# A bidirectional mLSTM and pooling block on one core: the head of the program rebuilt

## The chip, the cores and the metric

The kernel runs on one core of a Trainium2 chip. The metric is the device time of one execution, in microseconds (us). The engines are TensorE (PE, with PEld for its weight loads), VectorE (DVE), ScalarE (ACT), GpSimd (POOL) and SyncE (SP), which here only issues DMAs.

## The reference, cut to what matters

One layer of a hybrid diffusion backbone is computed in float32 for 128 context tokens and 1024 latent tokens, 1152 in all, of width 1024:

```python
mod = jnp.dot(jax.nn.silu(cond), w_ada) + b_ada
sh1, sc1, gt1, sh2, sc2, gt2 = [m[:, None, :] for m in jnp.split(mod, 6, axis=-1)]
h = _rmsnorm(x, g_pre_mix) * (1 + sc1) + sh1
z = jnp.einsum('bld,de->ble', h, w_in)
q, k, v, o, ig, fg, u, ga, gb = jnp.split(z, IN_SPLIT_POINTS, axis=-1)
log_f = jax.nn.log_sigmoid(fg + b_f)          # and log_i = ig + b_i, per direction and head
...                                            # two mLSTM directions, pooling mixer, merge, w_out
x = x + gt1 * _rmsnorm(y, g_post_mix)
...                                            # ConvFFN with sh2, sc2, gt2
```

`cond` is `c_ctx` for the context tokens and `c` for the latent ones, so `mod` has two columns of 6144 numbers. Nothing of the layer can be multiplied by `w_in` before `sh1` and `sc1` exist, which are the first 2048 numbers of `mod` (16 tiles of 128). The gate rows `ig` and `fg` go through two running scans over all tokens before the mLSTM can start.

## The kernel before, in words

Every large product is made of three matmuls: each float32 operand is split into a high and a low part, and hi·hi, hi·lo and lo·hi are added in PSUM. A **unit** is 128 output columns of a weight: 8 steps over the depth `k`, for 3 blocks of 384 tokens, so 24 steps of three matmuls. ACT makes the high part of a unit's weight (`hi_split`, into `ring_hi`), DVE the low part (`lo_split`, into `ring_lo`), into a ring of 3 slots. The semaphore `lo_ready` counts the low parts, `done0` the blocks that PE has finished, `evac0` the blocks that have been read out of PSUM, and `take0(q)` makes PE wait until the PSUM bank that block `q` writes is free again (`evac0` at least `q - 2`).

The **units in order** are set by the list `mains`: the gates, four of `u` (the pooling mixer's input), two of `v`, then `q` and `k` of head 0; after these nine (`SEG`) the attention of four heads runs between the units that follow. The order within an engine is the order of the code.

The **head** is what runs before unit 0. SP issues all its loads on one queue: the identity, block 0 of x, group 0 of the first modulation columns (`adaw`, 4 groups of 512 columns, 2 MB each, each group as two halves of 4 `k`), 13 small vectors into `vecs` (the last of them `c_ctx` and `c` and the conv weights), groups 1 and 2, blocks 1 and 2 of x, group 3, some constants, then the weights. PE transposes `vecs`, DVE copies the result to `vT`, and ACT takes silu of its last 16 columns as `condT`. PE then holds two columns of `condT` still and streams 512 columns of `adaw` past them (L741, 4 groups of 8), ACT copies each result row to `ada_row`, and 16 narrow transposes (L746) turn the rows into columns of 128 in PSUM bank 7. ACT squares and sums x (`x_stats`, L1098), DVE scales it (`scale_x`, L1451); `first_coef` (L1438, L1440) adds the bias and makes `coefA1`. Only then can ACT read the transposed x out of PSUM with the modulation (L1125, `norm_evac`), and DVE split it into `H_hi` and `H_lo` (L1464, L1401).

Unit 0, the gates, runs block by block while x is transposed for the block after (`first_norm`, L725). ACT then adds the gate bias to its three blocks and takes Abs, Exp and Ln (L1206 to L1212, `log_f_ready`); DVE makes the scans and sums in `gates()` (L1477 to L1511), which ends at `gate_rows_ready`. PE transposes those rows (L871, L873) at the end of unit 2.

The other 32 tiles of the modulation are made later, one to a unit from unit 2 on: DVE multiplies and adds a 128 x 1024 tile of `w_ada` (`ada_products`, L1571 and L1575), and PE sums it over the partitions with two matmuls against `ones` (`ada_sum`, L719) ahead of the unit's own matmuls. The wait of `ada_sum` is

```python
pe.wait_ge(ada_summed, a - ADA0 + 1)
```

and DVE's first such tile is made inside `gates()`, the second after `gates()` has ended.

## Time and profile before

| | us |
|---|---|
| median of 3 runs | 1965.92 (1962.02 to 1967.28) |
| the profiled execution, its span | 1965.6 |
| PE busy in the span | 1897.3 |
| DVE busy | 1026.7 |
| ACT busy | 628.3 |

The execution's own time is its span of 1965.6 us; what lies around it is within 0.4 us of the median. The page of the profile cuts the span into 40 equal slices of 49 us. In the first PE is 6 tenths busy and DVE 1 tenth, in the third PE's granted clock is 9 tenths, and from the fourth to the 39th nearly every slice shows PE at 9 tenths or more. The head and what follows it, up to 117 us, is therefore the part to look at closely.

### The profile page before, as it was taken

The numbers are of one execution on the slowest core, as the hardware profiler recorded it, in microseconds if no ns is written. First come the engines' busy times: TensorE is split into PE (matmuls) and PEld (weight loads), VectorE is DVE, ScalarE is ACT, GpSimd is POOL, SyncE is SP. The second block draws the span as 40 slices with busy tenths as digits, with TensorE's granted clock in tenths as the row PEclk, the third lists the DMA queues.
The fourth block names the chain that finished last, engine by engine and source line by source line (L and its number), as shares of the span: only waits on it lengthen the run. The fifth ranks groups of instructions, "written<-read, shape, count | busy, mean of one in ns | idle before, by whom it ended". The sixth has DMA issues, their size and how long they took to land.

```text
span 1965.6 us, 26936 instructions
## 1 busy us (share of the span) xinstructions
PE 1897.3 (97%) x10465; PEld 1772.4 (90%) x10465; DVE 1026.7 (52%) x2241; ACT 628.3 (32%) x1133; POOL 86.2 (4%) x125
## 2 busy tenths in 40 slices
PE   6999999999999999999999899999999999999995
PEld 1889999999999999999988899989989989989984
DVE  1853555555545333364545555555555555555556
ACT  2723222233234243361334442323223223223222
POOL 1000000000000000010000100000000000000003
PEclk9989999999999999999999899999999999999998
DMA  9133223323333233274222111111111111111104
GB/s 334 33 93 101 71 65 101 98 68 116 100 78 112 87 89 130 87 260 154 93 89 90 61 44 43 44 43 37 48 43 32 51 45 32 43 34 52 43 32 171
DMA packets 165370, 164.41 MB, mean 84 GB/s; under 512 B 5816, under 2 KB 141524, under 8 KB 165284
## 3 DMA queue, kind: packets, MB, share of 16 engines
q1 hardware_dynamic: 150532, 108.36, 18.8%
q0 software_dynamic: 10432, 37.17, 5.4%
q10 hardware_dynamic: 4320, 17.70, 2.2%
q8 instruction: 58, 0.95, 0.2%
q14 instruction: 28, 0.23, 0.0%
HBM read 131.48 MB, written 31.72 MB: 83 GB/s over the span
## 4 chain that ended last, share of the span: by engine, by line
PE 86%; DVE 5%; ACT 3%; issue 3%; DMA 2%; POOL 0%; SPq 0%; DVEq 0%; ACTq 0%; POOLq 0%
PE ps L696 20%; PE ps L698 20%; PE ps L697 20%; PE ps L929 5%; PE ps L1000 3%; PE ps L1002 3%; PE ps L1001 3%; PE ps L809 2%; PE ps L812 2%; PE ps L811 1%; PE ps L741 1%; DMA x1ld<-z_x 1%; PE ps L788 1%; DVE H_lo L1401 1%; ACT Wt L1179 1%
## 5 line engine op out<-in xcount | busy, mean ns | idle before, releaser
L696 PE MATMUL ps<-H_hi,ring_hi 128*128 128x384 f32 x2328 | 798.3, 343 | 5.0 <-DVE H_lo L1401 4.1
L697 PE MATMUL ps<-H_lo,ring_hi 128*128 128x384 f32 x2328 | 781.5, 336 | 0.0
L698 PE MATMUL ps<-H_hi,ring_lo 128*128 128x384 f32 x2328 | 781.4, 336 | 0.0
L696 PEld LDWEIGHTS ps<-H_hi,ring_hi 128*128 128x128 f32 x2328 | 439.7, 189 | 8.3 <-DVE H_lo L1401 4.7
L697 PEld LDWEIGHTS ps<-H_lo,ring_hi 128*128 128x128 f32 x2328 | 439.7, 189 | 1.6
L698 PEld LDWEIGHTS ps<-H_hi,ring_lo 128*128 128x128 f32 x2328 | 439.3, 189 | 0.0
L1771 DVE TENSOR_TENSOR acc<-ps,acc 128x512 f32<-128x512 f32 x198 | 135.0, 689 | 103.1 <-PE ps L1002 103.1
L1401 DVE TENSOR_TENSOR ring_lo<-raw,ring_hi 128x1024 fp32r<-128x1024 f32 (+1 forms) x129 | 152.1, 1188 | 55.4 <-ACT ring_hi L1085 48.1
L1000 PE MATMUL ps<-ring_hi,fT_hi 128*128 128x512 f32 x396 | 157.4, 397 | 12.5 <-DVE acc L1771 10.1
L1001 PE MATMUL ps<-ring_lo,fT_hi 128*128 128x512 f32 x396 | 155.2, 392 | 0.0
L1002 PE MATMUL ps<-ring_hi,fT_lo 128*128 128x512 f32 x396 | 155.1, 392 | 0.0
L1743 DVE SCALAR_TENSOR_TENSOR conv_g<-ps,vT,conv_g 128x378 f32<-128x378 f32 (+2 forms) x176 | 86.1, 510 | 121.9 <-ACT conv_g L1356 117.3
L1545 DVE SCALAR_TENSOR_TENSOR Cst<-Cst,Et,ps 128x257 f32<-128x257 f32 x64 | 30.9, 483 | 222.2 <-PE ps L812 222.2
L1085 ACT ACTIVATE ring_hi<-raw 128x1024 fp32r<-128x1024 f32 x66 | 68.2, 1049 | 214.5 <-PE ps L1002 212.6
L1575 DVE SCALAR_TENSOR_TENSOR ada_part<-raw,condT,ada_part 128x128 f32<-128x128 f32 x448 | 120.3, 344 | 0.0
L1743 DVE SCALAR_TENSOR_TENSOR conv_v<-ps,vT,conv_v 128x378 f32<-128x378 f32 (+2 forms) x176 | 86.1, 510 | 44.9 <-ACT conv_v L1356 40.2
L1000 PEld LDWEIGHTS ps<-ring_hi,fT_hi 128*128 128x128 f32 x396 | 74.7, 189 | 36.5 <-DVE acc L1771 19.0
L456 ACT ACTIVATE stage<-ps 128x384 f32<-128x384 f32 x72 | 35.2, 488 | 211.1 <-PE ps L698 211.1
L1002 PEld LDWEIGHTS ps<-ring_hi,fT_lo 128*128 128x128 f32 x396 | 74.8, 189 | 16.0
L1001 PEld LDWEIGHTS ps<-ring_lo,fT_hi 128*128 128x128 f32 x396 | 74.7, 189 | 14.6
L1057 ACT ACTIVATE ring_hi<-raw 128x1024 fp32r<-128x1024 f32 (+1 forms) x63 | 63.2, 1008 | 75.1 <-PE ps L698 57.3
L1361 ACT ACTIVATE fT_hi<-conv_v 128x384 fp32r<-128x384 f32 x66 | 34.7, 525 | 142.4 <-DVE conv_v L1760 142.4
(232 smaller groups left out, 1951.9 us busy)
## 6 DMA issues: line engine op xcount, KB each, us to landing
raw<-in_w_in_dram SPq DMA_DIRECT2D x44, 512.0 KB, 4.0
raw<-in_w_up_dram SPq DMA_DIRECT2D x44, 512.0 KB, 3.8
raw<-in_w_ada_dram SPq DMA_DIRECT2D x32, 512.0 KB, 5.0
raw<-in_w_down_dram SPq DMA_DIRECT2D x22, 512.0 KB, 3.8
adaw<-in_w_ada_dram SPq DMA_DIRECT2D x8, 1024.0 KB, 13.6
z_o<-stage ACTq DMA_DIRECT2D x8, 576.0 KB, 2.8
z_ga<-stage ACTq DMA_DIRECT2D x8, 576.0 KB, 2.8
z_gb<-stage ACTq DMA_DIRECT2D x8, 576.0 KB, 2.8
```

The lines of the kernel that those rows point to most:

```text
L696: pe.matmul(out, whi, xhi, start=first, stop=False)
L697: pe.matmul(out, whi, xlo, start=False, stop=False)
L698: return pe.matmul(out, wlo, xhi, start=False, stop=last)
L929: mm = pe.matmul(ps[:, bank + hb, :], x[:, k, tok], w[:, hb * 512:(hb + 1) * 512], start=(n == 0 and first), stop=(n == KD - 1 and last))
L1000: pe.matmul(out, fT_hi[:, slot, k, tok], ring_hi[:, r, cols], start=(k == 0), stop=False)
L1001: pe.matmul(out, fT_hi[:, slot, k, tok], ring_lo[:, r, cols], start=False, stop=False)
L1002: mm = pe.matmul(out, fT_lo[:, slot, k, tok], ring_hi[:, r, cols], start=False, stop=(k == 1))
L1085: act.activation(ring_hi[:, r, :], raw[:, n0 % RS, :], ACT.Copy).then_inc(hi_ready, 1)
L1401: return dve.tensor_tensor(out, full, hi.bitcast(F32), ALU.subtract)
L1575: ins = dve.scalar_tensor_tensor(out=part, in0=w, scalar=condT[:, cond, k:k + 1], in1=part, op0=ALU.mult, op1=ALU.add)
L1743: return dve.scalar_tensor_tensor(out=out, in0=src, scalar=vcol(w + NF * half + f, i), in1=out, op0=ALU.mult, op1=ALU.add)
L1771: dve.tensor_tensor(acc[:, t, cols], ps[:, 6 + hb, :], acc[:, t, cols], ALU.add).then_inc(evac2, 1)
```

## The change

The conditioning vectors `c_ctx` and `c` and the identity are loaded first, on ACT's queue, into a tile of their own (`cvec`), and PE transposes these 16 rows alone. SP's loads now go: group 0, x block 0, group 1, eleven vectors, group 2, x block 1, group 3, x block 2.

The groups are divided. **Groups 0 and 2** are multiplied and added by DVE (`ada_group`: 16 operations of 128 x 512 each), and PE sums them over the partitions with 8 matmuls of one column against `ones` (`ada_wide_sums`). **Groups 1 and 3** are made by PE with the 128 x 128 pieces of `adaw` held still and two columns of `condT` streamed (`ada_direct`: 32 matmuls to a group, 16 to a half). The row copies and the narrow transposes are gone.

The first **three units** are now gates, q and k of head 0, in this order (`RU = 3`), and they run block by block: all three for block 0, all three for block 1, all three for block 2. ACT reads them out with `ramp_evac`, and takes Abs, Exp and Ln after block 2 of the gates. The later tiles of the modulation start at unit 3 instead of unit 2, `gates()` takes the first of them, and the gate rows are transposed at the end of unit 4. Both `v` units now stand last before `SEG`, and both of their transposes follow the second (`v_turns`).

```diff
-    mains = [("gates", 0)] + [("u", g) for g in range(4)]
-    mains += [("v", 0), ("v", 1), ("q", 0), ("k", 0)]
+    mains = [("gates", 0), ("q", 0), ("k", 0)] + [("u", g) for g in range(4)]
+    mains += [("v", 0), ("v", 1)]
...
+    RU = 3
-    for s in range(2, NM):
+    for s in range(RU, NM):
...
+    def v_turns(m):
+        before = [mains[m - 1][1]] if m and mains[m - 1][0] == "v" and m != SEG else []
+        return before + ([mains[m][1]] if m == SEG - 1 else [])
...
+    def main_q(m, b):
+        return RU * b + m if m < RU else 3 * use_of[("main", m)] + b
...
+            ada_load(0)
             x_load(0)
-            ada_load(0)
+            ada_load(1)
...
-            for g in range(1, AG):
-                if g == AG - 1:
-                    x_load(1)
-                    x_load(2)
-                ada_load(g)
+            ada_load(2)
+            x_load(1)
+            ada_load(3)
+            x_load(2)
...
             pe.wait_ge(ident_in, 16)
+            pe.wait_ge(cond_in, 32)
+            pe.transpose(ps[:, 2, 0:16], cvec[0:16, :], ident[0:16, 0:16]).then_inc(cond_rows, 1)
...
+            def ada_direct(g, kh):
+                pe.wait_ge(ada_in[2 * g + kh], 16)
+                for a in range(4 * g, 4 * g + 4):
+                    for k in range(kh * KD // 2, (kh + 1) * KD // 2):
+                        mm = pe.matmul(ps[:, 7, 2 * ADA0 * kh + 2 * a:2 * ADA0 * kh + 2 * a + 2],
+                                       adaw[:, g, k, (a % 4) * P:(a % 4 + 1) * P], condT[:, :, k],
+                                       start=(k % (KD // 2) == 0), stop=(k % (KD // 2) == KD // 2 - 1))
+            def ada_wide_sums(g):
+                pe.wait_ge(ada_wide_mac, 2 * KD * (g // 2 + 1))
+                for a in range(4 * g, 4 * g + 4):
+                    for cond in range(2):
+                        mm = pe.matmul(ps[:, 7, 2 * a + cond:2 * a + cond + 1],
+                                       ada_wide[:, g // 2, cond, (a % 4) * P:(a % 4 + 1) * P], ones[:, :], start=True, stop=True)
...
+            for b in range(NB):
+                for m in range(RU):
+                    if b == 0:
+                        pe.wait_ge(lo_ready, m + 1)
+                    take0(main_q(m, b))
+                    for k in range(KD):
+                        if b == 0 and m == 0 and k < KD - 4:
+                            first_norm(0, k + 4)
+                        if b + 1 < NB and m and k % 2 == 0:
+                            if m == 1 and k == 0:
+                                pe.wait_ge(x_scaled, TB * (b + 2))
+                            first_norm(b + 1, (m - 1) * KD // 2 + k // 2)
+                        if m == 0:
+                            pe.wait_ge(h_split_done, b * KD + k + 1)
...
-                if m == 2:
+                if m == RU + 1:
                     pe.wait_ge(gate_rows_ready, 1)
...
             act.wait_ge(coef1, 1)
-            for b in range(NB):
-                norm_evac(lambda w: ps[:, 3 + w % 4, :], lambda w: act.wait_ge(xt_done, w + 1), xt_free, coefA1, 0, 0, tsc, 4, b)
+            first_evac(0)
+            hi_split(1)
+            x_stats(2)
+            hi_split(2)
+            first_evac(1)
+            for m in range(RU):
+                ramp_evac(m, 0)
+            first_evac(2)
+            for m in range(RU):
+                ramp_evac(m, 1)
+            ramp_evac(0, 2)
+            hi_split(3)
...
+            scale_x(0)
+            dve.wait_ge(vec_done, 1)
+            dve.tensor_copy(vT[:, :], ps[:, 1, 0:NV]).then_inc(vec_done, 1)
+            ada_group(2)
+            scale_x(1)
             first_coef()
...
+            norm_split(0, tsc, 4, 0)
+            lo_split(1)
+            scale_x(2)
+            lo_split(2)
+            norm_split(0, tsc, 4, 1)
+            norm_split(0, tsc, 4, 2)
```

**On PE, from the first instruction to the first product of unit 0.** Before (a run of equal rows for `ada_in1` to `ada_in7` stands where the line is left out; `ada_in` counts the halves of the groups):

```order
L711 MATMUL ps<-ident,vecs 128x108 [waits vectors_in,ident_in]
L712 MATMUL ps<-ident,vecs 128x88
L713 MATMUL ps<-ident,vecs 128x88
L741 MATMUL ps<-adaw,condT 2x512 [waits ada_in0,cond_done]
L741 MATMUL ps<-adaw,condT 2x512 x3
...
L746 MATMUL ps<-ident,ada_row 128x2 [waits row_read] x16
L725 MATMUL ps<-ident,X_96 128x128 [waits x_scaled]
```

Now, with L747 `ada_direct`, L757 `ada_wide_sums` and L732 the transposes of x:

```order
L720 MATMUL ps<-ident,cvec 128x16 [waits cond_in,ident_in]
L747 MATMUL ps<-condT,adaw 128x2 [waits ada_in2,cond_done]
...
L765 MATMUL ps<-ident,vecs 128x92 [waits vectors_in]
...
L757 MATMUL ps<-ones,ada_wide 128x1 [waits ada_wide_mac,pool_seq]
...
L732 MATMUL ps<-ident,X_97 128x128 [waits x_scaled]
...
L747 MATMUL ps<-condT,adaw 128x2 [waits ada_in6]
...
L757 MATMUL ps<-ones,ada_wide 128x1 [waits ada_wide_mac]
...
L747 MATMUL ps<-condT,adaw 128x2 [waits ada_in7]
```

The transpose of `vecs` has moved behind all of group 1, and group 3 stands in two halves around the sums of group 2.

**On ACT, from the last reads of the gates to the two functions of their logarithm.** Before:

```order
L1206 ACTIVATE Gt_97<-ps,gbias 36x384 [waits done0]
L1207 ACTIVATE Gt_98<-ps,gbias 36x384
L1210 ACTIVATE Gt_99<-Gt_98 36x1152 [waits evac0]
L1211 ACT_TABLE_LOAD
L1211 ACTIVATE Gt_99<-Gt_99 36x1152 [waits act_seq]
L1212 ACT_TABLE_LOAD
L1212 ACTIVATE Gt_99<-Gt_99 36x1152 [waits act_seq]
L1057 ACTIVATE ring_hi<-raw 128x1024 [waits done0,landed0]
```

Now (the gates' reads are L1170 and L1171, those of q and k L1173 and L1175):

```order
L1173 ACTIVATE qT_66<-ps 128x384 [waits done0]
L1175 ACTIVATE kT_67<-ps 128x384 [waits done0]
L1170 ACTIVATE stage_76<-ps,gbias 36x384 [waits done0]
L1171 ACTIVATE stage_77<-ps,gbias 36x384
L1089 ACTIVATE ring_hi<-raw 128x1024 [waits done0,landed2]
L1192 ACTIVATE Gt_98<-stage_77 36x1152 [waits evac0]
L1193 ACT_TABLE_LOAD
L1193 ACTIVATE Gt_98<-Gt_98 36x1152 [waits act_seq]
L1194 ACT_TABLE_LOAD
L1194 ACTIVATE Gt_98<-Gt_98 36x1152 [waits act_seq]
L1173 ACTIVATE qT_66<-ps 128x384 [waits done0]
```

The logarithm now stands behind the reads of q and k of blocks 0 and 1 and behind one more `hi_split`.

**On DVE, the end of `gates()` and the tile of the modulation that comes after it.** Before:

```order
L1511 CAST YS<-Gt_104 36x1152
L1401 TENSOR_TENSOR GS<-Gt_102,GS 36x1152 [waits dve_seq]
L1401 TENSOR_TENSOR YS<-Gt_104,YS 36x1152
L1571 TENSOR_SCALAR ada_part<-raw,condT 128x128 [waits ada_used,landed1]
L1571 TENSOR_SCALAR ada_part<-raw,condT 128x128
L1575 SCALAR_TENSOR_TENSOR ada_part<-raw,condT,ada_part 128x128 [waits ada_mac] x14
```

Now:

```order
L1594 CAST YS<-Gt_103 36x1152
L1454 TENSOR_TENSOR GS<-Gt_101,GS 36x1152 [waits dve_seq]
L1454 TENSOR_TENSOR YS<-Gt_103,YS 36x1152
L1654 TENSOR_SCALAR ada_part<-raw,condT 128x128 [waits ada_used,landed2]
L1654 TENSOR_SCALAR ada_part<-raw,condT 128x128
L1658 SCALAR_TENSOR_TENSOR ada_part<-raw,condT,ada_part 128x128 [waits ada_mac] x14
```

The rows are alike, but the tile was the one that unit 3 waited for, and is now the one that unit 4 waits for.

## Rows read from the trace of the kernel before

**Rows 1.** The page's first two parts: busy time, and granted clock by slice
```profile
PE 1897.3 (97%) x10465; PEld 1772.4 (90%) x10465; DVE 1026.7 (52%) x2241; ACT 628.3 (32%) x1133; POOL 86.2 (4%) x125
PEclk9989999999999999999999899999999999999998
```
**Rows 2.** Busy time by stretch: length, then each engine, clock, DMA share, GB/s
```profile
100.00:120.00 20.00, 15.27 (x87) 14.97 (x87) 17.96 (x41) 5.53 (x12) 3.19 (x6) 0.74 0.41 114
```
**Rows 3.** Waits of PE, 0 to 260 us: total, times, longest
```profile
PE ps L871 <- DVE YS L1401: 2.6, 1, 2.6
PE ps L719 <- DVE ada_part L1575: 2.1, 1, 2.1
```
**Rows 4.** Timeline of the head: start, length, engine, line, operation, count
```profile
20.03 30.14 PE L741 MATMUL ps<-adaw,condT 128*2 128x512 f32 x64 [0.79 <-ACT condT L1089]
...
50.10 0.91 PE L746 MATMUL ps<-ident,ada_row 2*128 2x2 f32 x12
...
52.47 2.42 PEld L725 LDWEIGHTS ps<-ident,X 128*128 128x128 f32 x12
...
54.06 0.17 DVE L1440 SCALAR_TENSOR_TENSOR coefA<-modT,vT 128x16 f32<-128x16 f32 x1
...
55.61 0.56 DVE L1401 TENSOR_TENSOR H_lo<-tsc,H_hi 128x384 fp32r<-128x384 f32 x1
```
**Rows 5.** DMA from 0 to 60 us in 40 slices of 1.5 us
```profile
GB/s 0 167 330 396 389 385 391 299 348 349 272 300 388 391 391 385 386 395 404 412 412 407 404 391 386 386 397 367 308 291 287 121 0 0 0 11 0 0 0 0
```
**Rows 6.** Timeline of PE around two of the sums over partitions
```profile
89.86 0.50 PE L719 MATMUL ps<-ones,ada_part 128*128 128x1 f32 x4
90.22 0.42 PE L696 MATMUL ps<-H_hi,ring_hi 128*128 128x384 f32 x1
...
111.82 0.99 PE L719 MATMUL ps<-ones,ada_part 128*128 128x1 f32 x4 [2.15 <-DVE ada_part L1575]
112.67 0.67 PE L696 MATMUL ps<-H_hi,ring_hi 128*128 128x384 f32 x1
```
**Rows 7.** Busy time and clock in single microseconds, columns as in Rows 2
```profile
53.00:54.00 1.00, 1.00 (x6) 1.00 (x5) 1.00 (x3) 0.00 (x0) 0.00 (x0) 0.50 0.08 16
...
116.00:117.00 1.00, 1.00 (x5) 1.00 (x5) 1.00 (x6) 0.67 (x1) 0.00 (x0) 0.50 0.65 181
```
**Rows 8.** Timeline of PE in unit 0: transposes of two steps in a row
```profile
60.28 0.49 PE L725 MATMUL ps<-ident,X 128*128 128x128 f32 x3
...
61.13 0.49 PE L725 MATMUL ps<-ident,X 128*128 128x128 f32 x3
```
**Rows 9.** Timeline of ACT: squares of x, high parts, logarithm of the gates
```profile
43.84 1.04 ACT L1098 ACTIVATE stage<-X 128x1024 f32<-128x1024 f32 x1
...
73.94 2.26 ACT L1057 ACTIVATE ring_hi<-raw 128x1024 fp32r<-128x1024 f32 x2
...
79.55 1.17 ACT L1210 ACTIVATE Gt<-Gt 36x1152 f32<-36x1152 f32 x1
...
84.52 1.17 ACT L1212 ACTIVATE Gt<-Gt 36x1152 f32<-36x1152 f32 x1
```
**Rows 10.** Timeline of DVE: scaling of x, a tile of products, the gates
```profile
48.02 2.08 DVE L1451 TENSOR_SCALAR X<-X,stat 128x1024 f32<-128x1024 f32 x3
...
80.95 3.76 DVE L1575 SCALAR_TENSOR_TENSOR ada_part<-raw,condT,ada_part 128x128 f32<-128x128 f32 x14
85.72 1.35 DVE L1485 SCALAR_TENSOR_TENSOR Gt<-Gt,Gt 36x1152 f32<-36x1152 f32 x1 [1.00 <-ACT Gt L1212]
...
106.14 1.34 DVE L1401 TENSOR_TENSOR YS<-Gt,YS 36x1152 fp32r<-36x1152 f32 x1
```
**Rows 11.** Timeline of ACT: reads of two blocks in a row of unit 2
```profile
98.82 0.49 ACT L456 ACTIVATE work<-ps 128x384 f32<-128x384 f32 x1 [3.46 <-PE ps L698]
102.99 0.49 ACT L456 ACTIVATE work<-ps 128x384 f32<-128x384 f32 x1 [3.67 <-PE ps L698]
```
**Rows 12.** Timeline of PE: after the transpose of the first v unit
```profile
182.03 0.60 PE L719 MATMUL ps<-ones,ada_part 128*128 128x1 f32 x4 [0.40 <-ACT vaug L1154]
```

More of the change, by code:

```diff
@@ L748, in _ @@
+            ada_direct(1, 1)
+            pe.wait_ge(vectors_in, 16 * 11)
+            pe.transpose(ps[:, 1, 0:92], vecs[0:92, 0, :], ident[0:92, 0:92])
+            pe.transpose(ps[:, 1, 92:180], vecs[0:88, 1, :], ident[0:88, 0:88])
+            pe.transpose(ps[:, 1, 180:268], vecs[0:88, 2, :], ident[0:88, 0:88]).then_inc(vec_done, 1)
+            pe.wait_ge(pool_seq, 7)
+            ada_wide_sums(0)
             pe.wait_ge(x_scaled, TB)
-            for k in range(KD):
+            for k in range(4):
@@ L1422, in rows, with ada_group @@
                 return vT[:, col:col + n].unsqueeze(2).to_broadcast([P, n, 2])
[L1424 to L1425 removed]
+            def ada_group(g):
+                n = g // 2
+                for k in range(KD):
+                    if k % (KD // 2) == 0:
+                        dve.wait_ge(ada_in[2 * g + k // (KD // 2)], 16)
+                    for cond in range(2):
+                        done = 2 * KD * n + 2 * k + cond
+                        part = ada_wide[:, n, cond, :]
+                        if k == 0:
+                            ins = dve.tensor_scalar(part, adaw[:, g, k, :], condT[:, cond, k:k + 1], None, ALU.mult)
+                        else:
+                            dve.wait_ge(ada_wide_mac, done - 1)
+                            ins = dve.scalar_tensor_tensor(out=part, in0=adaw[:, g, k, :], scalar=condT[:, cond, k:k + 1], in1=part,
+                                                           op0=ALU.mult, op1=ALU.add)
+                        ins.then_inc(ada_wide_mac, 1)
+            dve.wait_ge(cond_done, 1)
+            ada_group(0)
             dve.wait_ge(small_in, 16 * 9)
```

167 lines of the change are left out of this document (78 added, 89 removed).

## The prediction

> **What bounds the kernel now.** I read the page first [rows 1]: PE has work in 97% of the span at full clock nearly throughout, so a change at the head is worth what it takes from PE's start or from its later waits. The windows and the waits of PE show two places before 117 us. The first is the start. PE streams `adaw` from 20.03 to 50.2, `coefA1` is ready at 54.06 + 0.17 = 54.23, and the first product of unit 0 follows the first `H_lo` at 56.2 or later [rows 4]. The 64 records of L741 lie without a gap, 0.43 us each for most of them, so PE sets that stretch. The DMA moved 5.4 MB by 18 us and had moved nearly all of its 16.4 MB by 46 us [rows 5]: it is the floor under a faster start. The second place is 105 to 117 us. PE waits 2.6 us for the gate rows and 2.1 us for a tile of products [rows 3], and then runs at half clock until 117 [rows 2, 7].
>
> The sum has two parts: when `coefA1` is ready (call it C, 54.23 before), and how much PE loses after C.
>
> **The start: when C falls.** Cut are 30.1 us of L741 and some 2 us of row copies and narrow transposes. Added on PE are 64 matmuls of `ada_direct` and 16 of `ada_wide_sums`. A float32 matmul is recorded as two passes (L719: 2 matmuls, 4 records), so 160 passes, each with its own weights. The nearest row is L719, with the same 128 x 128 weights and one column: 4 passes in 90.22 - 89.86 = 0.36 us at full clock, 0.09 each; and 112.67 - 111.82 = 0.85 us at half clock, 0.21 each [rows 6]. The last of these may hold a little waiting for the weight behind it, so I take 0.20. That makes 32.0 us cold or 14.4 us warm.
>
> Which of the two it is decides the case. The granted clock fell to 0.50 after PE had done the narrow transposes L746 and waited (50.1 to 52.1), and again around 107.5 after a wait, and the narrow gate transposes did not bring it back; it rose behind wide transposes at 55 to 56 and behind products at 117 [rows 4, 7]. The new head gives PE, after an idle start, only operations that stream one or two columns, with 12 transposes between them. I take the half clock, 1.2 GHz, as nearest to L746. The Trainium skill ("TensorE: Matmul & The Clock Gate", Part 4) says that transposes do not bring the full clock; the trace disagrees, since it rose to 1.00 at 56 behind L725 alone. By the page the head would stay cold the more surely; by the trace the 12 transposes could give back up to some 3 us.
>
> PE begins when the first half of group 1 lands. Ahead of it in SP's queue are group 0 (2.10 MB) and block 0 of x (1.57), with it 1.05, and about 0.7 of small loads from the other queues: 5.4 MB. Before, that much had moved at 18.0 [rows 5]; the small vectors that slowed two of those slices now come later, so 17.5. From there PE has no gap: group 1, 12.8 us, to 30.3; three transposes of the vectors, 0.8; sums of group 0, 3.2; 12 transposes of x at 2.42/12 = 0.2 us, 2.4 [rows 4]; group 3 first half, 6.4, to 43.1; sums of group 2, 3.2; group 3 second half, 6.4, to 52.7. The four small operations of `first_coef` take some 0.9. C = 53.6, or 0.6 us earlier than before.
>
> DVE must keep up. A 128-column operation of the same form costs 3.76/14 = 0.27 us, a 1152-column one 1.35 against 0.34 alone, so 0.98 ns a column [rows 10]; 512 columns come to 0.65, and a group to about 9.9 us (an estimate from these rows). Group 0 runs 6.5 to 16.4 while the loads come in and is hidden. Group 2 cannot start before `vT`, which is behind PE's group 1: 31.1 + 0.6, to 41.6. PE wants it at 43.1, so DVE is just hidden; x block 1 is scaled (2.1 us) behind it while PE finishes. ACT's new loads issue beside SP's and are hidden too: `condT` is wanted by DVE at about 6 and by PE at 17.5. Were c late by 5 us, DVE's slack before 31 would take it.
>
> **After C: the three units.** A block of a unit is 102.99 - 98.82 = 4.17 us, a unit about 12.4 [rows 11]. Three transposes of x cost PE 61.13 - 60.28 - 3 x 0.172 = 0.34 [rows 8]. Work up to the end of three units: 3 x 12.4 + 20 x 0.34 = 44.0.
> - First product at C + 1.95 as before [rows 4]. Steps of unit 0 in block 0 come every 0.86 (DVE's cast and subtraction), so it ends at C + 8.5, 1.05 over its work.
> - q needs its low part: ACT's `hi_split` (2.26 for two, 1.1 each [rows 9]) only after its last read of block 0, some 0.9 before the last product, at C + 7.6, then DVE 1.2: C + 9.9. Loss 1.4. It ends at 15.4.
> - k needs its own: behind three squares and a root (3 x 1.04 [rows 9] with gaps and the root, about 3.6), DVE's small steps for the root and the scaling of x block 2 (2.08 [rows 10], 2.8 in all) and a subtraction: C + 16.2. Loss 0.8. It ends at 21.7.
> - Block 1 of the gates needs bank 0 free, and ACT reads it only behind all of `first_evac(1)`, whose last input is PE's last transpose: C + 23.1. Loss 1.4. The same again at block 2, C + 39.5. Loss 1.3.
> Sum of losses 1.95 + 1.05 + 1.4 + 0.8 + 1.4 + 1.3 = 7.9; three units end at C + 51.9. The gates end at C + 43.6.
>
> **After C: the logarithm and the tile behind it.** Before, Abs began at 79.55, C + 25.3 [rows 9]. Now block 2 of the gates ends only at C + 43.6. From there: ACT reads it and makes a high part, 2.4, then Abs to Ln, 84.52 + 1.17 - 79.55 = 6.1 [rows 9]: C + 52.1. DVE's `gates()` from the logarithm to the last row: 106.14 + 1.34 - 85.72 = 21.8 [rows 10]: C + 73.9. Then the tile for unit 4, 4.3 (107.5 to 111.8, [rows 6, 10]): C + 78.2. PE has meanwhile only unit 3, ready at 51.9 + 0.4 + 12.4 = C + 64.7, and stands in `ada_sum` of unit 4, with every later matmul behind it: **a wait of 13.5 us**. This long a wait drops the clock, as the shorter one at 105 did, and the 4.3 us from 112.7 to 117.0 that it then took to rise cost 2.15. The wait for the gate rows, now at the end of unit 4, is gone.
>
> PE's loss after C is now 7.9 + 13.5 + 2.15 = 23.5. Before it is the time from 54.2 to 117.2, 63.0, less the work in it: 44.0, pool products 2.1, gate transposes 1.3, two `ada_sum` 0.7, 14 matmuls of unit 3 2.4, in all 50.5: 12.5. The change costs 11.0 here. The two v transposes now follow each other with ACT's reads between them: before one of them cost 0.4 of waiting and some slower spacing [rows 12]; I add 1.0, with 0 and 2 as ends. Total: -0.6 + 11.0 + 1.0 = +11.4 on 1965.6, which with the 0.3 around it is 1977.3. It stands against the median 1965.9 as it is.
>
> **The rivals.**
> - **The head runs warm.** PE is then waiting for loads: group 3 needs 12.6 MB, at 36 us [rows 5]. DVE: `vT` at 24.5, group 2 to 34.4, x block 1 to 37.4. PE: first half of group 3 by 36, sums and second half by 39.5 to 40. C about 41, 13.2 earlier; with 12.0 after it, -1.2: 1964.7. The Trainium skill (same page, "Why this matters for your kernels") says that PE kept busy without a break gets the full clock; no row shows it for operations this narrow. For it: the passes lie back to back. Against it: L746, and the gate transposes.
> - **Part of the head warm,** through the 12 transposes or in a stretch of group 1: C 44 to 50, so 4 to 10 earlier than before, +2 to +8: about 1971.
> - **Faster.** The price after C is too high: if the tile of unit 4 did not hold PE (13.5 and 2.15 gone) and the head were warm, 1949. The reason would be that PE does not reach `ada_sum` of unit 4 by C + 65, or that DVE takes the tile before the gates are done; the order of both engines speaks against it. A milder form is a warm head with the losses of the ramp 5 us lower: 1960.
> - **Slower still.** A pass in the head costs 0.21 and DVE falls behind: 1.6 us more on PE, and group 2 ends at 43 and moves the second half: 1980 to 1983. It decides from the point where `vT` comes later than 33.
>
> **How the numbers follow.** Chances: cold head 0.58, with 1973 to 1983 as its own range; partly warm 0.15; warm 0.20; faster by a smaller price after C 0.07. The differences that a measurement of this kernel can tell are those over 0.3%, 5.9 us. Faster (below 1960.0) gets the last case and a little of the warm one: 0.09. Within 0.3% (to 1971.8) the rest of the warm one, half of the partly warm one and a little of the cold: 0.29. Slower 0.62. The range leaves out the fast case and the far end of the slow one: 1961 to 1982.
>
> **What would show it.** Right: a granted clock near 0.5 in most of 20 to 52 us, `coefA1` at 51 to 55, one wait of PE for `ada_part` of 12 to 15 us after unit 3, and a half clock of some 4 us behind it. Wrong in the first term: L747 at 0.09 us a pass, `coefA1` near 41. Wrong in the second: unit 4 starting within 3 us of unit 3's end. A late `condT` would show as DVE idle until after 8 us, without moving the end.

## The result and the profile after

Five runs of the changed kernel gave 1983.35 us in the median (1974.25 to 1987.89), five of the kernel before on the same chip 1966.5 (1962.02 to 1968.95). The ratio is 1.0083, with a 95% interval of 1.0059 to 1.0107: slower by 0.6 to 1.1%. The direction is as forecast. The median lies 1.35 us above the range's top of 1982, so the range did not hold it. The profiled execution is the median one: its time is 1983.35 and its span 1981.4, so 1.95 us lie around the span. In every execution for which both figures are known it is 1.7 to 3.0; one of the kernel before with a span of 1965.6 took 1967.36. The forecast added 0.3, since it held the span of one execution against the median of three. Note the spread too: 13.6 us over five runs, 6.9 before.

The page of the changed kernel, its first part, the row of the granted clock and the queue that brings instructions (packets, MB, share):

```profile
span 1981.4 us, 27134 instructions
PE 1897.8 (96%) x10546; PEld 1796.1 (91%) x10546; DVE 1046.9 (53%) x2275; ACT 627.6 (32%) x1129; POOL 86.8 (4%) x125
...
PEclk9989999999999999999999999999999999999998
...
q8 instruction: 85, 1.39, 0.3%
```

The fourth slice, 149 to 198 us, looks as before. The third, 99 to 149, is the low one, 8 tenths here and before [rows 1], and the list of PE's waits up to 260 us says why (total, times, longest):

```profile
PE ps L726 <- DVE ada_part L1658: 13.1, 1, 13.1
PE ps L747 <- DMA adaw<-in_w_ada_dram: 10.6, 1, 10.6
PE ps L720 <- DMA ident<-in_consts_dram: 7.8, 1, 7.8
PE ps L705 <- ACT stage L1171: 2.6, 2, 1.3
```

The 2.6 us for the gate rows and the 2.1 us for a tile of [rows 3] are gone, and one wait of 13.1 stands in their place. (The 10.6 and 7.8 are the wait for the first loads.) The head, PE and then DVE, answering to [rows 4]:

```profile
18.61 13.78 PE L747 MATMUL ps<-condT,adaw 128*128 128x2 f32 x64 [10.56 <-DMA adaw<-in_w_ada_dram]
...
32.74 3.48 PE L757 MATMUL ps<-ones,ada_wide 128*128 128x1 f32 x16
36.08 2.80 PE L732 MATMUL ps<-ident,X 128*128 128x128 f32 x12
38.67 6.83 PE L747 MATMUL ps<-condT,adaw 128*128 128x2 f32 x32
45.36 3.55 PE L757 MATMUL ps<-ones,ada_wide 128*128 128x1 f32 x16
48.77 6.97 PE L747 MATMUL ps<-condT,adaw 128*128 128x2 f32 x32
```

```profile
32.98 0.44 DVE L1530 COPY vT<-ps 128x268 f32<-128x268 f32 x1 [8.24 <-PE ps L767]
33.34 0.88 DVE L1487 TENSOR_SCALAR ada_wide<-adaw,condT 128x512 f32<-128x512 f32 x2
34.13 9.36 DVE L1491 SCALAR_TENSOR_TENSOR ada_wide<-adaw,condT,ada_wide 128x512 f32<-128x512 f32 x14
...
56.27 0.17 DVE L1515 SCALAR_TENSOR_TENSOR coefA<-modT,vT 128x16 f32<-128x16 f32 x1
```

A pass takes 13.78 / 64 = 0.215 us, PE is without a gap from 18.6 to 55.7, and `coefA1` is ready at 56.44, 2.2 us later than before. So the head that was rebuilt to be shorter is no shorter. The first sign of the forecast, a granted clock near 0.5 in most of 20 to 52 us, did not show: the record reads 1.00 there and on to 125. That the passes ran at half clock is read from what one costs (0.21 us at a recorded 0.50, 0.09 at 1.00 [rows 6]) and is tested by e2 and e7 below. Further on, the chain behind the gates: the logarithm on ACT, the last row and the tile on DVE, the sums of unit 4 on PE, and the granted clock (the last number but two of a window):

```profile
102.55 1.15 ACT L1192 ACTIVATE Gt<-stage 36x1152 f32<-36x1152 f32 x1
...
107.50 1.17 ACT L1194 ACTIVATE Gt<-Gt 36x1152 f32<-36x1152 f32 x1
```

```profile
129.13 1.35 DVE L1454 TENSOR_TENSOR YS<-Gt,YS 36x1152 fp32r<-36x1152 f32 x1
130.50 0.48 DVE L1654 TENSOR_SCALAR ada_part<-raw,condT 128x128 f32<-128x128 f32 x2
130.91 3.75 DVE L1658 SCALAR_TENSOR_TENSOR ada_part<-raw,condT,ada_part 128x128 f32<-128x128 f32 x14
```

```profile
134.81 0.98 PE L726 MATMUL ps<-ones,ada_part 128*128 128x1 f32 x4 [13.07 <-DVE ada_part L1658]
```

```profile
125.00:130.00 5.00, 0.00 (x0) 0.00 (x0) 4.92 (x5) 0.00 (x0) 0.00 (x0) 0.68 0.01 2
130.00:135.00 5.00, 0.19 (x1) 0.23 (x2) 4.97 (x18) 0.00 (x0) 3.20 (x6) 0.50 0.18 49
135.00:140.00 5.00, 5.00 (x18) 5.00 (x19) 4.89 (x18) 1.06 (x1) 0.00 (x0) 0.50 0.78 212
```

DVE is busy throughout the time in which PE stands still: the tile is short (4.2 us), but it queues behind the whole of `gates()`. One more place lay where I had not looked, in the FFN loop far behind the head (`pe.Fori` in the code, a loop whose instructions the engine runs several times over). PE's waits from 230 us on, the row put down to issue, two pieces of the chain of work that ended last, and the matmuls on both sides of the first of them:

```profile
PE ps L705 <- issue: 3.9, 2, 2.1
```

```profile
1477.36 2.08 issue
...
1781.47 1.78 issue
```

```profile
1476.97 0.39 PE L1034 MATMUL ps<-ring_hi,fT_lo 128*128 128x512 f32 x1
1479.44 0.43 PE L705 MATMUL ps<-H_hi,ring_hi 128*128 128x384 f32 x1 [2.08 <-issue]
```

In these PE waits for nothing that another engine or a load does. L1034 is the last line of the loop's body on PE and L705 does the first product of its next pass, so the stall lies at the loop's return. The kernel before has no such row behind 230 us, and 58 packets in its instruction queue against 85.

### The profile page after: what moved, and what is told of

Its sections match the earlier page's. It is cut to its first block, busy times and chain, and to the rows that moved or that the text cites. A ratio compares the mean times of both kernels' runs of the same rounds, so it can differ in the third digit from the quotient of the medians.

```text
span 1981.4 us, 27134 instructions
## 1 busy us (share of the span) xinstructions
PE 1897.8 (96%) x10546; PEld 1796.1 (91%) x10546; DVE 1046.9 (53%) x2275; ACT 627.6 (32%) x1129; POOL 86.8 (4%) x125
## 3 DMA queue, kind: packets, MB, share of 16 engines
q1 hardware_dynamic: 150356, 108.28, 18.7%
## 4 chain that ended last, share of the span: by engine, by line
PE 88%; DVE 6%; ACT 3%; issue 1%; DMA 1%; SPq 0%; POOL 0%; DVEq 0%; ACTq 0%
PE ps L705 20%; PE ps L707 20%; PE ps L706 20%; PE ps L961 5%; PE ps L1032 4%; PE ps L1033 4%; PE ps L1034 4%; PE ps L842 2%; PE ps L845 2%; PE ps L844 1%; PE ps L747 1%; PE ps L821 1%; PE ps L732 1%; DMA adaw<-in_w_ada_dram 1%; DVE acc L1852 1%
## 5 line engine op out<-in xcount | busy, mean ns | idle before, releaser
L705 PE MATMUL ps<-H_hi,ring_hi 128*128 128x384 f32 x2328 | 798.5, 343 | 13.4 <-DVE H_lo L1454 4.1
L705 PEld LDWEIGHTS ps<-H_hi,ring_hi 128*128 128x128 f32 x2328 | 439.3, 189 | 18.8 <-issue 7.7
L1034 PE MATMUL ps<-ring_hi,fT_lo 128*128 128x512 f32 x396 | 154.4, 390 | 0.0
L1034 PEld LDWEIGHTS ps<-ring_hi,fT_lo 128*128 128x128 f32 x396 | 74.3, 188 | 16.0
```

Source lines behind the costliest of these rows:

```text
L705: pe.matmul(out, whi, xhi, start=first, stop=False)
L1034: mm = pe.matmul(out, fT_lo[:, slot, k, tok], ring_hi[:, r, cols], start=False, stop=(k == 1))
```

## A mark that splits the time

To compare runs I split the span at two points: `coefA1` ready (C), and the first matmul of the attention scores (ps<-maskbf,idbf), which follows the segment that the change reorders. In the changed kernel, and in e8 below:

```profile
227.39 0.23 PE L818 MATMUL ps<-maskbf,idbf 128*128 128x128 bf16 x1
```

```profile
209.70 0.23 PE L822 MATMUL ps<-maskbf,idbf 128*128 128x128 bf16 x1
```

Every kernel of the study by these points (us; head = C, middle = from C to the mark, rest = from the mark to the end of the span; packets = those of the instruction queue):

| kernel | median (range, runs) | head | middle | rest | packets |
|---|---|---|---|---|---|
| before | 1966.5 to 1967.1 in five comparisons (2.2 to 7.9, 5 to 29) | 54.2 | 159.6 | 1751.7 | 58 |
| changed | 1983.35 (13.6, 5) | 56.4 | 171.0 | 1754.0 | 85 |
| e1_no_tile4 | 1970.30 (9.9, 10) | 56.6 | 154.7 | 1756.2 | 76 |
| e2_warm | 1976.84 (5.1, 4) | 53.9 | 170.9 | 1751.0 | 59 |
| e3_both | 1963.03 (5.2, 10) | 53.1 | 155.9 | 1750.1 | 59 |
| e4_head_alone | 1974.18 (14.0, 10) | 54.6 | 159.6 | 1762.8 | 94 |
| e5_pad | 1980.16 (2.4, 5) | 54.8 | 170.9 | 1750.3 | 59 |
| e6_before_pad | 1975.93 (17.0, 12) | 55.5 | 159.7 | 1759.0 | 85 |
| e7_hot | 1970.38 (11.6, 12) | 57.2 | 155.6 | 1757.3 | 87 |
| e8_no_tile4_pad | 1965.45 (4.2, 11) | 54.6 | 155.1 | 1752.6 | 59 |
| e9_rows | 1955.23 (2.8, 5) | 46.4 | 155.7 | 1750.4 | 59 |
| e10_before_pad147 | 1968.53 (3.7, 10) | 56.7 | 159.2 | 1750.7 | 59 |
| e11_head_alone_pad | 1968.04 (3.8, 11) | 56.5 | 159.4 | 1750.7 | 59 |
| e12_rows_no_wide | 1953.51 (3.5, 5) | 45.4 | 154.6 | 1752.4 | 59 |

Read it by columns. The middle has three values, one for each arrangement: about 159.5 with the old order of units, 155.5 with the new one, 171 with the new one and the tile for unit 4. The rest is 1750.1 to 1752.6 in every kernel with 58 or 59 packets and 1754 to 1763 in every one with 76 or more. The head varies by 2 us between profiles of kernels whose heads do the same (e4 and e11: 54.6 and 56.5), so a difference of 2 us there is not told by one profile. (In e6 and e10 the head is later for a reason of its own: their added matmuls stand behind the transposes of `vecs`, and the first pass of L741 starts at 21.02 and 23.35 in place of 20.03.)

The loop itself gives a cleaner split than the rest. PE goes from a last matmul like L1034 to a first one like L705 nine times in it, and every second time is a return of the loop (each pass of the body has two such parts). The gap there is 0.22 or 0.23 us, or, at some of the four returns, 2.2 to 3.0. The time is from the first of the nine to the last; packets are those of the instruction queue from 1150 to 1900 us:

| profiles | returns that stall | loop, us | packets |
|---|---|---|---|
| before, e2, e3, e5, e8 to e12 | 0 of 4 | 603.4 to 603.6 | 6 or 7 |
| e1 | 2 | 609.6 | 24 |
| e7 | 3 | 611.5 | 33 |
| changed | 3 | 612.3 | 34 |
| e6 | 3 | 613.0 | 33 |
| e4 | 4 | 615.2 | 42 |

A return that stalls costs some 3 us and comes with some 9 packets. Within 12 us of each of the 15 stalled returns lie 4 packets; within 12 us of the other returns (looked at in the changed kernel, before, e1, e5, e6, e7 and e10) lie none or one. In the changed kernel the stalled returns are at 1324.6, 1479.4 and 1783.3 us and the one at 1630.4 has neither stall nor packet. (The list of waits puts the first of the three down to DVE's `ring_lo`.) Around the loop the changed profile is shorter than before, by 4.1 us from the mark to the loop and by 2.5 behind it; what made it so is not known. That is why the column "rest" shows only 2.3 of the 8.9 us that the loop lost.

## The experiments

**Without the tile for unit 4 (e1).** The tile's products move one unit on, with all later ones.

```
-        if s - 2 not in NORM_AT and ADA0 + len(ADA_AT) < 48:
+        if s - 2 not in NORM_AT and s != RU + 1 and ADA0 + len(ADA_AT) < 48:
```

> The changed kernel with one edit: no tile of the modulation is made at unit 4, so the tiles from there on come one unit later. Theory A (order): the 13.1 us wait of PE ahead of unit 4 is DVE's queue, where the tile stands behind the gates. Without the tile the wait is gone, and with it the 2.1 us of half clock behind it; unit 4 starts within 2 us of unit 3's end, the gate rows are ready before unit 4 ends, and the time is 14 to 16 us under the changed kernel's, about 1968. Theory B (chain): PE would be held by the gates' chain anyway, at the gate transposes behind unit 4 or at the next tile; then a wait of 8 us or more appears there and the time falls by less than 5 us.

1970.3 us, ratio 1.0020 [1.0006, 1.0034], 13.1 us below the changed kernel where theory A had 14 to 16. The wait of 13.1 is gone, no other takes its place, and the middle falls from 171.0 to 154.7. The mechanism behind the largest term stands. But the rest of the span grew, which no theory of mine held; that led to e5 and e6.

**A warm head (e2), and both (e3).** Matmuls of a constant bf16 tile (448 columns) run ahead of group 1 (42), ahead of group 3 (12), and one after every fourth narrow matmul of group 1 and of the first half of group 3.

```
+            wide(42)
             pe.wait_ge(cond_done, 1)
-            ada_direct(1, 0)
+            ada_direct(1, 0, 4)
```

> The changed kernel, with wide bf16 matmuls of 448 columns added on PE whose result nobody reads: 42 before the first pass of group 1, one behind each 4 direct matmuls of groups 1 and 3 (first half), 12 before group 3. Theory A (clock): the passes of the head run at 1.2 GHz because PE did nothing wide before them. With the wide ones a pass takes 0.09 us in place of 0.213, and coefA1 is ready at 42 to 47 in place of 56.4; the wait before unit 4 stays near 13; the time falls by 9 to 13 us, to about 1971. Theory B (pass): a pass of this form costs 0.2 us at any clock, bound by its weights; then coefA1 comes at 60 or later, and the time rises by 4 or more.

> Both edits at once: no tile at unit 4, and the wide matmuls in the head. If the two costs are apart, as theory A has it, the time falls by the sum, 23 to 28 us under the changed kernel, to about 1958, and beats the kernel before by some 8. If they share a cause (the gates' chain would take up what the head gives), it falls by no more than the larger of the two, about 15.

1976.84, ratio 1.0063 [1.0041, 1.0085], and 1963.03, ratio 0.9988 [0.9978, 0.9997]. The timeline of PE in e2_warm, and its granted clock in two windows:

```profile
18.54 1.02 PE L752 MATMUL ps<-condT,adaw 128*128 128x2 f32 x8 [0.88 <-DMA adaw<-in_w_ada_dram]
19.42 0.35 PE L745 MATMUL ps<-warm 128*128 128x448 bf16 x1
...
22.89 0.53 PE L745 MATMUL ps<-warm 128*128 128x448 bf16 x1
23.22 1.71 PE L752 MATMUL ps<-condT,adaw 128*128 128x2 f32 x8
```

```profile
18.00:22.00 4.00, 3.46 (x31) 3.49 (x32) 3.30 (x8) 1.19 (x2) 0.00 (x0) 0.99 1.09 345
22.00:26.00 4.00, 4.00 (x20) 3.93 (x21) 1.97 (x3) 0.00 (x0) 0.00 (x0) 0.50 1.05 366
```

Eight passes cost 19.42 - 18.54 = 0.88 at first, 0.11 each, at a granted clock of 0.99, and 24.78 - 23.22 = 1.56 further on, 0.20 each, at 0.50. The price of a pass is a matter of the clock, and the clock did not stay up, so C came at 53.9 and not at 42 to 47. The theory of the price holds; that so few wide matmuls would hold the clock was wrong. The time fell by 6.5 us where 9 to 13 were expected, and 3.3 of them are the wide matmuls' own (e5 to e2 below); the other 3.2 came with the end of the stalls. With both edits it fell by 20.3, between the theories' 23 to 28 and 15: the two costs are apart, but the head's was not won back.

**The new head alone (e4).** The units, the ramp and the orders of ACT and DVE behind the head are those of the kernel before.

```
-    mains = [("gates", 0), ("q", 0), ("k", 0)] + [("u", g) for g in range(4)]
-    mains += [("v", 0), ("v", 1)]
+    mains = [("gates", 0)] + [("u", g) for g in range(4)]
+    mains += [("v", 0), ("v", 1), ("q", 0), ("k", 0)]
...
-    RU = 3
+    RU = 1
```

> The new head with the old ramp: loads, split of the modulation columns and coefficient as in the changed kernel; the order of units, unit 0 alone block by block, and the later tiles as in the kernel before. Theory A: the head alone costs the 2.2 us by which coefA1 is later (56.4 against 54.2), so the time is 1967 to 1971, and the other 11 us of the change belong to the three units block by block. Theory B: the cold head harms what comes after it as well; then it is 1975 or more.

1974.18, ratio 1.0038 [1.0021, 1.0056]. Its mark is at 214.2, 0.3 us from that of before, so head and middle together cost nothing; in the profiled execution (1978.78, 4.6 over the median) 11 us came from the rest, with four issue stalls there of 2.0 us at most, 7.6 in all. Behind two of the four the granted clock is 0.50 for 2 to 3 us (1315.9 to 1318.9, 1623.5 to 1625.5), which is most of what is left of the 11. Theory A's 1967 to 1971 and theory B's 1975 both miss: the head does no harm to what follows it, and the loop does.

**The place of the loop (e5, e6, later e10, e11).** What the kernels with stalls had in common was about the same number of PE instructions ahead of the FFN loop. So I changed that number alone, by matmuls of two columns before the first group. They change no result. In the new head they fall into PE's idle time; in the kernel before, where they come behind the transposes of `vecs`, 81 of them take 2.35 us and 147 take 4.11.

```
+            pe.wait_ge(pool_seq, 8)
+            for _ in range(66):
+                pe.matmul(ps[:, 1, 0:2], warm[:, 0:P], warm[:, 0:2], start=True, stop=True)
             pe.wait_ge(cond_done, 1)
```

> The changed kernel, with 66 bf16 matmuls of 128 x 2 columns added on PE ahead of group 1, where PE is idle (8 to 18.6 us). They change no result and no wait; they only move every later PE instruction by the same number of places as the 66 wide ones of the run e2_warm did. Theory (place of the loop): the 1.8 to 2.3 us stalls put down to issue in the FFN loop, which cost after, e1 and e4 some 2.3, 4 and 11 us behind the first attention score, come from where the loop's body lies in PE's instruction stream; at the place it had in e2_warm there is none. Then the profile shows no issue wait of PE behind 230 us, about 59 packets of the instruction queue, the first attention score stays at 227.4 +/- 0.5, the median is about 1978 (e2_warm was 1976.8 with a first score 2.6 us earlier) and the runs lie within 4 us of each other. Rival (the stalls belong to the change's work or to chance, not to the place): issue stalls as in the changed kernel, 75 packets or more, median 1980 to 1985 and a spread over 8 us.

> The kernel before, with 81 bf16 matmuls of 128 x 2 columns ahead of its group 0, where PE is idle. No result, no wait changed. A float32 matmul counts as two passes, so this moves the FFN loop about as far along in PE's instruction stream as the new head does (80 float32 matmuls and 16 transposes there against 32 and 35 before). Theory (place of the loop): issue stalls of about 2 us appear in the loop, more than 70 packets of the instruction queue, the time rises by 2 to 8 us to 1969 to 1975 and the spread widens, with nothing at the head moved. Should the place be off by a few instructions the stalls may be fewer. Rival (stalls belong to the new head's or ramp's work): no stall, 58 packets, 1966 to 1967.

In stalls, packets and spread both are as the theory of the place has it. The changed kernel with 66 more matmuls: 1980.16 in runs that lie within 2.4 us, ratio 1.0066 [1.0053, 1.0079], no stall, 59 packets. The median is 2 us above the theory's 1978, and the mark came at 225.67 in place of 227.4: this profile is the fastest of the five runs (1977.83; the others 1979.72 to 1980.18), with the head 1.6 us shorter. The kernel before with 81 more: 1975.93, 0.9 over the theory's range, ratio 1.0035 [1.0019, 1.0051], runs from 1962 to 1979, 85 packets, and behind 230 us this row among PE's waits (below it the rows of the instruction queue of e6_before_pad and of e10_before_pad147):

```profile
PE ps L697 <- issue: 5.7, 3, 2.1
```

```profile
q8 instruction: 85, 1.39, 0.3%
```

```profile
q8 instruction: 59, 0.97, 0.2%
```

Two controls followed. e10 gives the kernel before 147 such matmuls, which puts its loop where e5's lies; e11 gives e4 its 66.

> The kernel before with 147 padding matmuls in place of e6's 81, so that its FFN loop lies where it lay in e5 and e8. Theory (the place alone): no issue stalls, 59 packets of the instruction queue, 1966 to 1968 with a spread under 8 us. Rival (the padding matmuls themselves, or any shift, disturb the kernel): stalls as in e6_before_pad, 1970 to 1978.

> The new head with the old order of units and the old ramp (e4_head_alone) and the 66 padding matmuls. Theory (place): e4's 1974.2 with a spread of 14 us becomes 1967 +/- 1 with a spread under 6 us, the first attention score stays at 214.2 +/- 0.5, no issue stall. With e8 at 1965.5 and coefA1 2 us later there, the new ramp without the tile would then be worth 3 to 4 us. Rival (another cause): 1972 to 1976, stalls remain.

1968.53, ratio 1.0012 [1.0003, 1.0021], and 1968.04, ratio 1.0008 [0.9999, 1.0017]: no stall in either, spreads of 3.7 and 3.8 us. (e11's mark came at 215.86, not at 214.2, with the head 1.9 us later than e4's; e10 lies 1.7 us over before, and its head is 2.5 later.) More padding cured what less padding brought, so it is the place and not the padding. Four pairs that differ by padding alone, in the medians: 1983.35 - 1980.16 = 3.2 for the changed kernel, 1974.18 - 1968.04 = 6.1 for e4, 1975.93 - 1968.53 = 7.4 for before (a little low, since e10's padding makes its head 1.2 us later than e6's), 1970.30 - 1965.45 = 4.9 for e1. Three of the pairs, and perhaps all, were measured on two chips each; the medians of the kernel before in these comparisons agree within 0.6 us. The place decides whether returns can stall and not how many do: among e6's runs the fastest, 1962.09, lies under the median of before. This is the spread. e11 also gives the clean price of the new head: 1.2 us on 1966.8, which its interval does not tell from nothing.

**The tile at a good place (e8).** e1 with the 66 padding matmuls.

> The changed kernel without the tile of products for unit 4 (that of e1_no_tile4) and with the 66 padding matmuls of e5_pad. The difference to e5_pad is the clean price of the tile, without issue stalls if the place is what brings them. Theory (place, and the tile's wait of 13.1 us with the half clock behind it): 1978 - 15.2 = about 1963 to 1965, spread under 4 us, no issue stalls, first attention score at 211.3 +/- 0.5. Rival (no place effect): as e1_no_tile4, 1970 with a spread of 10 us. Rival (the wait only hides another one behind it): the first attention score is the same, but the time is under 10 us better than e5_pad.

1965.45, ratio 0.9992 [0.9983, 1.0001], within 4.2 us, and no stall; the mark, at 209.70 in place of 211.3, is early by the shorter head of this profile. The tile of unit 4 costs 1980.16 - 1965.45 = 14.7 us; the middle says 170.9 - 155.1 = 15.8, the wait of 13.1 and some 2.7 of half clock.

**A head kept warm by force (e7).** One wide matmul after every second narrow one; no tile for unit 4; on DVE group 2 ahead of the copy of `vT`.

```
                                        start=(k % (KD // 2) == 0), stop=(k % (KD // 2) == KD // 2 - 1))
+                        if every and (k + 1) % every == 0:
+                            wide(1)
```

> The changed kernel without the tile of products for unit 4; 44 two-column and 42 wide (448 columns, bf16) matmuls of a constant tile ahead of group 1, one wide one after every second narrow matmul of groups 1 and 3, and 12 ahead of group 3; on DVE group 2 stands ahead of the copy of vT, so that it doesn't wait for PE. Theory (the clock is what the narrow matmuls cost, and in e2_warm the wide ones were too few to hold it): passes stay at 0.10 us through groups 1 and 3, group 1 ends at about 28, group 2 on DVE at about 35, group 3 then waits for its loads until 34 to 36 and coefA1 is ready at about 46 (e3_both: 53.1, before: 54.2). The time is then about 1956. Rival 1: the clock falls again behind the first passes, each wide one costs 0.37 us, group 1 takes 14 + 6 = 20 us and coefA1 comes at 60: about 1970. Rival 2: with the head 7 us earlier the ramp loses it again to the loads of block 2 or of the weights: coefA1 at 46 but 1961 or more.

1970.38, ratio 1.0013 [1.0001, 1.0026]: rival 1 in its mechanism. That its 1970 came out is luck: C was 57.2 and not 60, and its profiled run has three stalled returns (87 packets), which cost 8 us in the loop and which the rival did not have. The timeline of PE, with the clock still up and after it has fallen:

```profile
18.70 0.50 PE L752 MATMUL ps<-condT,adaw 128*128 128x2 f32 x4
19.06 0.35 PE L745 MATMUL ps<-warm 128*128 128x448 bf16 x1
...
23.69 0.85 PE L752 MATMUL ps<-condT,adaw 128*128 128x2 f32 x4
24.40 0.53 PE L745 MATMUL ps<-warm 128*128 128x448 bf16 x1
```

PE has no gap from 18.7 to 56.8, a third of that time streams 448 columns, and still a pair of narrow matmuls goes from 0.36 to 0.71. The Trainium skill ("TensorE: Matmul & The Clock Gate", "Why this matters for your kernels") gives unbroken work as what brings and keeps the full clock; for narrow matmuls this run disagrees.

**Rows in place of columns (e9, e12).** If narrow passes are the trouble, PE's two groups should be done as the kernel before did all four: `condT` still, 512 columns of `adaw` streaming, a copy of the row, four turns. DVE keeps its two groups. e9 has 34 and 22 wide matmuls ahead of the two groups, e12 none; both have the loop at e5's place, group 2 ahead of `vT` and no tile for unit 4. (e7 had that order on DVE too, with the groups as columns, and its C was 57.2, so the order alone does not do it.) Both compute everything that the reference asks for.

```
-                        mm = pe.matmul(ps[:, 7, 2 * ADA0 * kh + 2 * a:2 * ADA0 * kh + 2 * a + 2],
-                                       adaw[:, g, k, (a % 4) * P:(a % 4 + 1) * P], condT[:, :, k],
+                    mm = pe.matmul(ps[0:2, bank, :], condT[:, :, k], adaw[:, g, k, :], start=(k == 0), stop=(k == KD - 1))
+                mm.then_inc(row_done, 1)
```

> The changed kernel without the tile for unit 4, and with PE's share of the head (groups 1 and 3) done the way of the kernel before: condT stands still and 512 columns of adaw stream, 16 matmuls of 2 passes, a copy of the row by ACT and 4 narrow transposes for each group. DVE keeps groups 0 and 2, group 2 ahead of the copy of vT. 34 wide constant matmuls ahead of group 1, 22 ahead of group 3, and 98 two-column ones, so that the FFN loop lies where it lay in e5 and e8. Theory (what the new head loses, it loses by streaming two columns under 128 x 128 weights: 0.213 a pass at half clock, 32 passes more in all, and no hold on the clock): group 1 takes 7 to 7.5 us from 18.6, group 3 starts when its loads land (34.3) and takes 7.5, coefA1 is ready at 44 to 45 (before 54.2, e8 56.6) and the time is 12 us below e8, about 1953.5. Rival 1 (loads set the head): group 3 lands at 38 or later, coefA1 at 48, 1957. Rival 2 (what is won at the head comes back in the ramp, where DVE, x block 2 or the weights of q and k are late): coefA1 at 44.5, but 1958 or more.

> e9_rows with its 56 wide constant matmuls (34 ahead of group 1, 22 ahead of group 3) replaced by two-column ones at the start, so the number of instructions ahead of the FFN loop is the same. In e9 coefA1 was ready at 46.35 and the time was 1955.23. Theory A (the wide ones are wanted, for each stream of rows starts at half clock without them): the first 7 passes of a group take 0.86 in place of 0.43, 3 us a group, and the narrow sums and turns between them run at half clock; group 3 starts at 36 to 37, coefA1 is ready at 48 to 49, the time is 1957 to 1958. Theory B (the wide ones are in the way): group 3 starts as soon as its loads land, at 34.3 to 35, the two effects cancel or better, coefA1 at 44.5 to 46.5, 1953.5 to 1955.5.

1955.23, ratio 0.9938 [0.9924, 0.9951], and 1953.51, ratio 0.9932 [0.9918, 0.9945]: both beat the kernel before and the changed one. The timeline of PE in e12_rows_no_wide, up to the turns that end the head:

```profile
20.29 9.94 PE L754 MATMUL ps<-adaw,condT 128*2 128x512 f32 x16 [8.05 <-DMA adaw<-in_w_ada_dram]
...
30.45 1.88 PE L769 MATMUL ps<-ones,ada_wide 128*128 128x1 f32 x16
...
32.60 2.48 PE L735 MATMUL ps<-ident,X 128*128 128x128 f32 x12
35.08 7.67 PE L754 MATMUL ps<-adaw,condT 128*2 128x512 f32 x16
42.68 1.95 PE L769 MATMUL ps<-ones,ada_wide 128*128 128x1 f32 x16
44.56 0.41 PE L761 MATMUL ps<-ident,stage 2*128 2x2 f32 x4
```

A group takes 7.7 to 9.9 us this way against 13.8 as columns. The narrow sums behind it still find the full clock (1.88 against 3.48): in e12 the granted clock is 1.00 from 30 to 32 us, while they run, and 0.75 from 32 to 34, so it fell behind them. C is 45.4, and what the head wins arrives at the end whole: e8 to e9, C 8.2 earlier, 10.2 us less in the medians. e9 missed its own forecast of 44 to 45 and 1953.5 (C 46.4, its second group behind the wide matmuls). Of e12's two theories B held, by its numbers (C 45.4, 1953.51). That e12 is faster than e9 is not shown: both profiles span 1952.4 us and the runs overlap. Group 1 started cold, 2.9 us longer than e9's 7.03, as A had it; but group 3 lost only 0.6 and began 1.6 us before e9's, whose 22 wide matmuls ran until 36.7, when the loads had landed (e12's second group starts at 35.08 without a wait).

## Why the prediction was off, point by point

**Rightly foreseen.** Narrow passes run at half clock, by their durations (the record of the clock did not show it). The chain behind the gates came out link by link: Abs at C + 46.1 (forecast 46.0), the last row at C + 74.0 (73.9), the tile at C + 78.4 (78.2). The wait before unit 4 was forecast at 13.5 and is 13.1; half clock behind it 2.15, some 2.7 by e5 and e8. From C on the forecast was +11.0 with +1.0 for the v turns; the middle is 170.95 against 159.64, +11.3. Both v turns are recorded at 219.67 and 221.55 with one wait of 0.5. The shares inside are right too: without the tile the new ramp wins 159.6 - 155.1 = 4.5 us, and the forecast's losses (7.9 and 1.0 against 12.5) had 3.6.

**Mis-sized: the head.** C was forecast at 53.6 and is 56.44, 2.8 later. The start, 18.61 for 17.5, is 1.1 of it. The pass is the rest: I took 0.20 where the row had 0.85 / 4 = 0.21 and put the difference down to a wait that does not exist; 160 passes of 0.215 are 2.4 us more than of 0.20, of which a little came back elsewhere. The rival "slower still" priced that at 1.6 and added a late DVE, which did not come here: DVE ended group 2 at 43.5 and PE wanted it at 45.4. One uncertainty I had not seen is the clock at group 3: its first half took 6.83 us in the changed kernel, e1 and e11, and 3.9 to 4.1 in e4, e5 and e8, with C 2 us apart. The 12 transposes ahead of it sometimes bring the clock up and sometimes don't; "partly warm" happens in some executions, at a fifth to a half of the size that I gave it. One reason that it is so small is DVE, which is late in just these:

```profile
43.48 3.57 PE L758 MATMUL ps<-ones,ada_wide 128*128 128x1 f32 x16 [0.88 <-DVE ada_wide L1495]
```

This is e8. PE is done with the half group 2.8 us sooner and then waits 0.88 for group 2 (0.77 in e5, 0.97 in e4), and the sums run at half clock again.

**Missing: the FFN loop.** The sum had no term behind 230 us, for the diff touches nothing there, and this is the step that failed: it put the rest of the program at nothing. In the profiled execution three of the loop's four returns stall, and it takes 612.3 us against 603.5 before. The padded twin e5, with the loop at another place and all else alike, is 3.2 us faster in the median, and its runs lie within 2.4 us in place of 13.6. Without this term, at e5's place, the change costs 13.3 us, 1980.2, inside the range.

**Missing: the time around the span.** The forecast added 0.3 us to its span and the profiled execution has 1.95, so 1.65 were left out.

The profiled execution is the median one, so its account closes: 1977.3 + 2.8 (C) - 0.7 (11.3 for 12.0) + 2.3 (from the mark to the end, made of 8.9 more in the loop and 6.6 less around it) + 1.65 = 1983.35. The excess over the range is 1.35 us. So had any one of the three terms been as forecast, the time would lie in the range. Two of them are sizes that were off; the loop is a mechanism that the sum did not have.

**Wrong in the rivals.** A warm head was given 0.20 and 1964.7, as though only the clock stood between the new head and a gain of 13 us. The chance was not absurd (a pass does cost 0.11 while the clock is up), but no kernel here held it up under narrow passes. Wide matmuls brought 2.4 to 3.3 us (e8 to e3, e5 to e2), and in e7 C was no earlier. Much of the gain was to be had, but by the form of the matmul.

**Open.** Why the loop stalls from one place and not from another: I tried the loop of before at its own place, 81 and 147 matmuls further on, and that of the changed kernel at three, and did not map it. The packets tie stall and instruction loading together return by return; that PE waits for these very packets is inferred, since no row names them as the releaser. Why one return of an execution stalls and the next does not is open too.

## What to carry to other kernels

Price a matmul by how it holds the clock as well as by its columns: two-column matmuls under 128 x 128 weights took 13.8 us a group where streaming 512 columns past two took 7 to 10. When a short step is put behind a long one on an engine (here the 4 us tile behind `gates()`), its price is the queue ahead of it, and moving it by one unit can be the whole difference. If a kernel's time spreads after an edit at its head, look for issue waits at the return of a later loop, count the packets of the instruction queue, and pad the instruction stream before judging the edit. And compare an execution's span with its own time, not with the median of others.

## What the runs showed of the hardware

- A hardware loop that is not touched can get slower by where it starts. In five kernels 2 to 4 of its four returns stall for 2.2 to 3.0 us, each with some 9 packets of the instruction queue more; the loop takes 609.6 to 615.2 us in them against 603.4 to 603.6 in the nine others. In the medians it is 3.2 to 7.4 us, with spreads of 10 to 17 against 2 to 5 (the kernel before: up to 7.9). Such a kernel has 76 to 94 packets in all, every other 58 or 59.
- Narrow float32 passes do not keep TensorE at its upper level of 2.4 GHz: in e2 the granted clock fell from 0.99 to 0.50 under them with no gap on PE, and in e7 it fell with 448-column matmuls in between for a third of the time. Nor did they bring it up: in the changed kernel 64 passes back to back take 13.8 us, 0.215 each, and those up to 55.7 us, with 15 transposes between them, no less.
- The record of the granted clock can miss a stretch at half clock. In the changed kernel it reads 1.00 from the start to 125 us, though 25 narrow passes fill each 5 us from 20 on, 0.20 a pass, which is the price at 0.50; the same in e5 from 20 to 35. In e12 it reads 1.00 while the passes of L754 go from 3 in 2 us (24 to 26) to 6 (26 to 28). In e7 the fall is recorded, as the rows below show (the last number but two). Before the first change on record the durations of the passes are what to read:

```profile
20.00:25.00 5.00, 5.00 (x36) 4.89 (x36) 3.77 (x8) 0.21 (x1) 0.00 (x0) 0.74 1.07 336
25.00:30.00 5.00, 5.00 (x26) 4.82 (x26) 4.05 (x7) 0.00 (x0) 0.00 (x0) 0.50 1.04 405
```
